# Retention in a two-model transformer kernel: from all-pairs scores to chunks of 128 tokens with carried states

## What is computed

```python
def retention_dir(q, k, v, log_gamma, include_diag):
    C = q.shape[-2]
    idx = jnp.arange(C, dtype=jnp.float32)
    rel = idx[:, None] - idx[None, :]
    ...
    decay_in = jnp.where(mask[None], jnp.exp(lg * jnp.maximum(rel, 0.0)[None]), 0.0)
    s = jnp.einsum('bhncd,bhnkd->bhnck', q, k) * decay_in[:, None]
    o_in = jnp.einsum('bhnck,bhnke->bhnce', s, v)
    k_dec = k * jnp.exp(lg * (C - 1 - idx)[None, :])...
    kv = jnp.einsum('bhncd,bhnce->bhnde', k_dec, v)
    ...
    def step(state, kv_n):
        return state * chunk_decay + kv_n, state
    ...
    q_dec = q * jnp.exp(lg * (idx + 1.0)[None, :])...
    o_x = jnp.einsum('bhncd,bhnde->bhnce', q_dec, s_prev)
    return o_in + o_x
...
    o = retention_dir(qc, kc, vc, log_decay[0], True) + flip(
        retention_dir(flip(qc), flip(kc), flip(vc), log_decay[1], False))
```

## Time and profile before

| | us |
|---|---|
| three runs, median (lowest to highest) | 3733.61 (3730.58 to 3734.66) |
| the profiled execution | 3733.86 |
| its span in the profile | 3732.0 |
| TensorE busy | 3615.1 (97%) |
| VectorE busy | 1887.5 (51%) |
| ScalarE busy | 1362.2 (36%) |
| GpSimd busy | 482.0 (13%) |
| mean granted TensorE clock | 0.991 of full |

### The profile page before, as it was taken

One profiled execution on the slowest core, in us unless ns is written; L12 is line 12 of the kernel. 1 busy time (PEld: TensorE's weight loads), 2 busy tenths in 40 slices (PEclk: granted clock), 3 DMA queues, 4 the chain that ended last, 5 costly groups with the idle time before them and its releaser, 6 DMA issues. The chain is left out here.

```text
span 3732.0 us, 58501 instructions
## 1 busy us (share of the span) xinstructions
PE 3615.1 (97%) x24178; PEld 3178.2 (85%) x24178; DVE 1887.5 (51%) x3312; ACT 1362.2 (36%) x2629; POOL 482.0 (13%) x586
## 2 busy tenths in 40 slices
PE   7999999999999999999999999999998999999998
PEld 6788778888888887888899889999997976888887
DVE  4555556565535556544455664433436556344444
ACT  3445444122224444322422452442233236244232
POOL 1222211000012432000110100110013110011001
PEclk9999999999999999999999999999999999999999
DMA  5111121333322212233311113222221111332332
GB/s 192 63 69 53 69 90 63 130 119 119 119 85 72 60 55 66 91 96 96 112 52 46 49 52 97 83 86 90 89 83 51 46 57 40 99 96 88 96 96 74
DMA packets 88248, 306.72 MB, mean 82 GB/s; under 512 B 10016, under 2 KB 13216, under 8 KB 87728
## 3 DMA queue, kind: packets, MB, share of 16 engines
q1 hardware_dynamic: 85184, 293.25, 24.5%
q0 software_dynamic: 2800, 9.73, 0.8%
HBM read 300.84 MB, written 2.10 MB: 81 GB/s over the span
## 5 line engine op out<-in xcount | busy, mean ns | idle before, releaser
L1944 DVE TENSOR_TENSOR weight_lo<-weight_raw,weight_hi 128x1024 fp32r<-128x1024 f32 (+1 forms) x464 | 561.4, 1213 | 431.9 <-ACT weight_hi L1344 431.3
L1344 ACT ACTIVATE weight_hi<-weight_raw 128x1024 fp32r<-128x1024 f32 (+1 forms) x464 | 476.7, 1031 | 587.9 <-PE bank L621 358.3
L621 PE MATMUL bank<-h_hi,weight_hi 128*128 128x512 f32 (+1 forms) x1288 | 469.1, 364 | 18.5 <-DVE h_lo L2387 9.1
L621 PE MATMUL bank<-h_lo,weight_hi 128*128 128x512 f32 (+1 forms) x1288 | 453.0, 352 | 0.0
L621 PE MATMUL bank<-h_hi,weight_lo 128*128 128x512 f32 (+1 forms) x1288 | 452.8, 352 | 0.0
L621 PE MATMUL bank<-u_hi,weight_hi 128*128 128x272 f32 (+2 forms) x1392 | 433.5, 311 | 3.0 <-DVE weight_lo L1944 2.1
L621 PE MATMUL bank<-u_lo,weight_hi 128*128 128x272 f32 (+2 forms) x1392 | 422.9, 304 | 0.0
L621 PE MATMUL bank<-u_hi,weight_lo 128*128 128x272 f32 (+2 forms) x1392 | 422.2, 303 | 0.0
L2810 POOL TENSOR_TENSOR scratch<-scratch 128x256 f32<-128x256 f32 (+2 forms) x132 | 113.8, 866 | 2020.5 <-ACT scratch L1382 2016.6
L621 PEld LDWEIGHTS bank<-h_hi,weight_hi 128*128 128x128 f32 x1288 | 245.9, 191 | 72.2 <-issue 31.2
L621 PEld LDWEIGHTS bank<-u_hi,weight_hi 128*128 128x128 f32 x1392 | 264.2, 190 | 30.4 <-issue 17.1
(11 more groups left out here) (319 smaller groups left out, 7983.7 us busy)
## 6 DMA issues: line engine op xcount, KB each, us to landing
weight_raw<-in_w_mlp SPq DMA_DIRECT2D x128, 512.0 KB, 3.6
weight_raw<-in_w_ff SPq DMA_DIRECT2D x128, 512.0 KB, 3.5
weight_raw<-in_w_in SPq DMA_DIRECT2D x92, 512.0 KB, 3.6
weight_raw<-in_w_mod SPq DMA_DIRECT2D x80, 512.0 KB, 4.4
weight_raw<-in_a_w_qkv SPq DMA_DIRECT2D x24, 512.0 KB, 3.9
weight_raw<-in_b_w_qkv SPq DMA_DIRECT2D x24, 512.0 KB, 3.6
first_weight<-in_w_mod SPq DMA_DIRECT2D x16, 512.0 KB, 15.2
weight_raw<-in_w_ret_o SPq DMA_DIRECT2D x16, 512.0 KB, 3.5
```

What stands on the lines that cost most here:

```text
L621: m = e.matmul(view[:, 0:hi - lo], a[:, k, :], b[:, k0 + k, lo:hi], start=(k == 0 and i == 0), stop=(k == kt - 1 and i == 2))
L1344: e.activation(whi[s % N_SPLIT][:, 0:kt, :], raw[n % N_RAW][:, 0:kt, :], ACT.Copy).then_inc(*tick("act_split", ("hi", n)))
L1944: e.tensor_tensor(wlo[s][:, 0:kt, :], raw[n % N_RAW][:, 0:kt, :], whi[s][:, 0:kt, :].bitcast(F32), ALU.subtract).then_inc(*tick("dve_split ...
```

## The change

Scores are computed only within a chunk: key tile j against its own 128 queries (16 for the meta tile). What lies between chunks goes through states. Per unit and direction ("way" 0 forward, 1 backward):

- `ret_turn` (TensorE): five transposes bring the keys of both heads to tokens in partitions.
- `ret_keys` (VectorE): three operations multiply them by their decays into KD and KDM.
- `ret_states` (TensorE): per chunk, way and head a matmul with the decayed keys stationary (64 columns wide) and the values moving; four chunks forward, and four (layer 0) or three (layer 1) backward.
- `ret_queries` (VectorE): three operations in layer 0, two in layer 1 make decayed queries QD, from factors QT that ScalarE makes in `query_decay`.
- `ret_states` (VectorE): eight (seven) operations in two chains, state i = state i-1 times the decay of a chunk plus the matmul's result.
- `ret_values` (TensorE): per chunk a matmul of the chunk's own scores (128 rows), then for each state that reaches it and each head a matmul of 64 rows with the state stationary.

The decays of a head shrink to 128 x 128, made after the fourth `fill()`. The six `fill()` calls of a unit stay, but stand between other parts. The constant table that is loaded is 624 columns narrower.

```diff
+                def ret_turn(g):
+                    e.wait_ge(*at("rr", layer, g, 1))
+                    for part, tiles in enumerate((ROW_TILES[0:4], ROW_TILES[4:5])):
...
+                            m = e.transpose(view[:, P * i:P * i + P], RK[:, g % 2, lo:lo + P], ident)
...
                 def ret_scores(g, span):
...
-                    for j, (k0, nk) in enumerate(ROW_TILES):
-                        views = [take("rs", layer, g, span, j, s) for s in range(2)]
+                    views = [take("rs", layer, g, span, s) for s in range(2)]
+                    for j, lo, n in tiles:
                         for s in range(2):
                             r = slice(HD * s, HD * s + HD)
-                            e.matmul(views[s][:, 0:hi - lo], RK[r, b, k0:k0 + P], RQ[r, b, lo:hi], start=True,
+                            m = e.matmul(views[s][:, lo - first:lo - first + n], RK[r, b, lo:lo + P],
+                                         RQ[r, b, lo:lo + n], start=True, stop=True)
...
+                def ret_states(g):
+                    b = g % 2
+                    e.wait_ge(*at("rvd", layer, g, 2))
+                    e.wait_ge(*at("kd", layer, g))
+                    for way, chunks in enumerate(((4, 0, 1, 2), (3, 2, 1, 0)[0:4 - layer])):
...
+                                m = e.matmul(view[c, P * i:P * i + P], key,
+                                             RV[b][0:P if j < 4 else N_META, j, P * s:P * s + P], start=True, stop=True)
...
+                def ret_values(g, span):
+                    first = tok.spans[span][0]
+                    views = [take("ro", layer, g, span, s) for s in range(2)]
+                    for s in range(2):
+                        e.wait_ge(*at("sd", layer, g, span, s))
+                    for way in range(2):
+                        e.wait_ge(*at("state", layer, g, way))
+                    e.wait_ge(*at("qd", layer, g))
+                    for j, lo, n in ret_tiles(layer, span):
+                        o = slice(lo - first, lo - first + n)
+                        for s in range(2):
+                            e.matmul(views[s][:, o], RV[g % 2][0:n, j, P * s:P * s + P], SD[0:n, span, s, o],
+                                     start=True, stop=False)
+                        ways = [(0, j)] * (j < 4) + [(1, 3 if j == 4 else 2 - j)] * (j != 3)
+                        for way, i in ways:
+                            for s in range(2):
+                                r = slice(HD * s, HD * s + HD)
+                                m = e.matmul(views[s][:, o], STATE[r, way, i, :], QD[r, way, lo:lo + n],
+                                             start=False, stop=(way, i) == ways[-1])
...
                 def ret_units(g, fill):
+                    ret_turn(g)
                     ret_scores(g, 0)
                     if g:
                         ret_broadcast(g - 1, 1)
...
-                    ret_values(g, 0)
+                    ret_states(g)
                     ret_scores(g, 1)
                     fill()
+                    ret_values(g, 0)
+                    fill()
                     ret_statistics(g, 0)
+                    ret_values(g, 1)
                     fill()
                     ret_broadcast(g, 0)
-                    fill()
-                    ret_values(g, 1)
                     fill()
                     ret_statistics(g, 1)
                     fill()
```

VectorE's unit, and the chain of states in it:

```diff
                 def ret_units(g, fill):
+                    ret_keys(g)
                     ret_decay(g, 0)
                     if g:
                         ret_normalise(g - 1, 1)
-                    if g < 3:
-                        decay_strip(2 * g + 2)
                     fill()
+                    ret_queries(g)
+                    ret_states(g)
                     ret_decay(g, 1)
+                    fill()
                     fill()
                     ret_variance(g, 0)
                     fill()
                     ret_normalise(g, 0)
-                    if g < 3:
-                        decay_strip(2 * g + 3)
-                    fill()
+                    for h in range(2 * g + 2, 2 * g + 4 if g < 3 else 0):
+                        decay_strip(h)
...
+                            if i == 0:
+                                e.tensor_scalar(STATE[:, way, 0, :], view, 1.0, None, ALU.mult).then_inc(
+                                    *tick("dve_attn", *done))
+                            else:
+                                e.wait_ge(*at("state", layer, g, way))
+                                e.scalar_tensor_tensor(
+                                    out=STATE[:, way, i, :], in0=STATE[:, way, i - 1, :],
+                                    scalar=CD[:, 4 * way + g:4 * way + g + 1], in1=view, op0=ALU.mult,
+                                    op1=ALU.add).then_inc(*tick("dve_attn", *done))
```

More of the change, by code:

```diff
@@ L478, in ret_var, with ret_tiles @@
             return RVAR[:, c:c + 6].rearrange("p (s t) -> p s t", s=2)
+        def ret_tiles(layer, span):
+            return [(j, *ROW_TILES[j]) for j in ([4] if (layer, span) == (0, 0) else []) + [2 * span, 2 * span + 1]]
         def ret_before(layer, g, span):
@@ L1126, in gate_retention @@
                     yield from product_T(("rg", layer, m_), (w_in, 16 + m_), U_HI, U_LO, wide(layer), ready)
+                def ret_turn(g):
+                    e.wait_ge(*at("rr", layer, g, 1))
+                    for part, tiles in enumerate((ROW_TILES[0:4], ROW_TILES[4:5])):
+                        job = ("kt", layer, g, part)
+                        view = take(*job)
+                        for i, (lo, _) in enumerate(tiles):
+                            m = e.transpose(view[:, P * i:P * i + P], RK[:, g % 2, lo:lo + P], ident)
+                        m.then_inc(*tick("pe_turn", job))
+                        close(*job)
@@ new lines, in ret_states @@
+                def ret_states(g):
+                    e.wait_ge(*at("cd", layer))
+                    for s in range(2):
+                        e.wait_ge(*at("ro", layer, g - 1, 1, s))
+                    for i in range(4):
+                        for way in range(2):
+                            last = 3 - layer * way
+                            if i > last:
+                                continue
+                            job = ("st", layer, g, way)
+                            view = view_of(*job)[:, P * i:P * i + P]
+                            e.wait_ge(*at(*job))
+                            done = [("state", layer, g, way)] + [("free", *job)] * (i == last)
+                            if i == 0:
[7 more added lines that the diff above has]
+                                    op1=ALU.add).then_inc(*tick("dve_attn", *done))
@@ L3010, in ret_units @@
                     for span in range(2):
-                        fill()
-                        fill()
+                        for _ in range(2 + (span == 0)):
+                            fill()
                         e.wait_ge(*at("rvar", layer, g, span))
```

174 lines of the change are left out of this document (126 added, 48 removed).

## The result

| | before | changed | ratio, 95% interval |
|---|---|---|---|
| median of the first comparison, us | 3732.9 (3730.6 to 3734.7) | 3695.1 (3691.0 to 3696.4) | 0.9895 [0.9883, 0.9908] |
| profiled execution, us | 3733.9 | 3696.2 | |
| span, us | 3732.0 | 3694.4 | |

Faster by 1.05%, 38 us where 43.4 were forecast.

A forecast was written before the change was run, and what follows sets the result against it. TensorE's stream was taken to bound the kernel: 120.3 us less 1.0 leaves, 75.9 us is added, a gain of 43.4 us. From 3733.9 that gives 3690.5, stated as 3690.0 us, range 3680 to 3706.

The forecast's parts named there:

- The bound: Both retention stages: TensorE's stream sets the time at upper clock, so time leaving it leaves the total absent new waits.
- The sum: Retention stages: TensorE work removed less work added, a gain of 43.4 us.
- What goes, 120.3 us: Old scores and values on TensorE in eight units: their busy times, 120.3 us, leave.
- The check by edges: Old scores and values, start to start plus group edges: 14.28 us, some 14.8 a unit, about 120 us in all.
- The 1.0 us that I reserved: First scores of layer 1: about 1 us is a bank VectorE frees late; the following product will meet it.
- What is added, 75.9 us: New TensorE work: pairs 34.3 us, full-array matmuls 15.8, transposes 4.4, switches of array tiling 21.4.
- A single matmul's latency as the drain: Alternative switch price from the skill page, some 166 ns drain: switches near 30 us, gain near 35, time near 3699.
- The signs: Expected in the changed profile: windows about 184 and 157 us, scores and values about 9.5 a unit, values 3.6 and 2.3.
- Rival 1: First values wait for VectorE's chain of states: 1 to 2 us a unit, 3698 to 3706 us; chance 0.13.
- Rival 2: New matmuls' stationary loads no longer hidden: 40 us more if none are, 3730 us, no measurable change; chance 0.04.
- Rival 3: TensorE waits every unit for keys, states, values chain; slower once the wait passes 5.4 us a unit; chance 0.02.
- What I costed at nothing: VectorE's and ScalarE's new work, PSUM banks, the smaller constant table and other stages: covered or unchanged, no added time.

The follow-up runs named there:

- second and third run: The changed kernel, unaltered, timed twice more beside the kernel before: medians 3689.4 and 3689.9 us, ratios 0.9885 and 0.9883.
- the queries six times: Changed kernel with VectorE computing the decayed queries six times instead of once, five into buffers nobody reads: 3700.7 us.
- Own chunk only: Changed kernel without the products of states and decayed queries, so nothing crosses from one chunk to another: 3665.5 us.
- the queries nine times: Changed kernel with VectorE computing the decayed queries nine times instead of once, eight into buffers nobody reads: 3746.8 us, ratio 1.0037 to the kernel before.
- the fill ahead of the transposes: Changed kernel with the first fill of products moved ahead of transposes and first scores in each layer's first unit: 3689.0 us.

## Why the prediction was right, and what was mis-sized

- **The bound.** Right: TensorE was busy for every microsecond of both windows, and the span fell by what left its stream (37.8 and 37.6 us).
- **The sum.** Forecast 43.4 us, found 37.8 in the windows: 5.6 short. The lengths of the units say where. The six units behind the first ones gave 28.9 us (4.27, 4.23 and 4.18 in layer 0, 5.40, 5.41 and 5.38 in layer 1), where the terms of the prediction, taken unit by unit, make 30.5. The two first units and the products ahead of them gave 8.9 us, where its terms make 12.8.
- **What goes, 120.3 us: right but for the first units.** In a unit behind the first the busy sum is what leaves. The check by edges came out low (14.28 and 0.2 us): the last value matmul reaches 0.19 us into the products, as the first of them takes 0.31 us from start to start (2016.27 to 2016.58) and not 0.12, and 0.09 is the entry, 14.76 in all. In the first units the scores were longer because the clock was at 0.50: from start to start their groups took 15.19 and 16.86 us, where 14.28 and 13.95 are usual. I let these 3.8 us leave with the matmuls, but for 1.0. But such a stretch does not leave with the matmuls that stand in it: it was 3.4 + 6.8 us long before and is 6.8 + 6.8 in the first run of the changed kernel, and slows transposes and products instead. The 3.4 us more cost **1.7 us**; in the second and third run they are not there. This is the term that was most mis-sized. The 1.0 us that I reserved as a wait for a bank was also misread: the row has 0.20 us of waiting, and the rest is this clock.
- **What is added, 75.9 us: some 2.5 us too small.** From start to start a unit has 9.97 us in layer 0 and 8.55 in layer 1. With four exits of 0.1 us and entries of 0.09 us (two in layer 0, one in layer 1), that is 10.55 and 9.04 us, 78.4 in all; against 14.76 and 14.43 before, this gives the 4.2 and 5.4 us by which the units are shorter. Full-array instructions at 0.111 and switches at 0.20 were measured within 0.005 us of what I took, and pairs at 0.107 (single starts give 0.112). What I did not count is the border between the meta keys' states (16 rows) and the others (128 rows), a switch once in each unit: the starts there are 0.20 and 0.16 us apart instead of 0.11, 0.15 us more, 1.2 us in all. A single matmul's latency as the drain, the estimate that the prediction makes from the page TensorE: Matmul & The Clock Gate of the Trainium skill (Single matmul latency), would have meant some 0.27 us a switch; the measured 0.20 us decides for the rows.
- **The signs.** The changed windows are 187.0 and 159.0 us, for 184 and 157 forecast. Values: 3.44 and 2.33 us for 3.6 and 2.3. Scores and values of a unit: 9.3 us on average from start to start, 9.8 with the edges that the forecast of 9.5 included.
- **How much of it is luck.** The later comparisons, 41.7 and 43.8 us below the kernel before, lie closer to 43.4 than the sum deserves: in the stages the change gives 40.2 and 39.5 us there, and the rest of the difference lies in stages that the change leaves alone.
- **Rival 1, VectorE late at the first values:** not there, no wait, and 2.6 to 3.5 us of slack in the eight units. The run with the queries six times shows that it was near: 4 us more on the chain and it begins.
- **Rival 2, loads not hidden:** refuted. Own chunk only has full-array instructions at 0.111 us and pairs at 0.107. In its trace full-array instructions of only 16 moving columns also start 0.112 us apart, which is then the load; and in the trace of before those of 256 columns start 0.216 us apart, so that 128 columns of stream are some 0.108 us. The rule of the Trainium skill (TensorE: Matmul & The Clock Gate, What overlaps and what doesn't), by which a load hides only behind matmuls on other rows of the array, is not what these full-array matmuls show: 0.111 us holds one load or one stream, not one after the other.
- **Rival 3, slower by a wait in each unit:** not there, but its price was wrong. I put the break-even at a wait of 5.4 us in each unit. The run with the queries nine times is slower than before with 3.7 us on average. A long wait costs the clock behind it as well: 29.5 us of waits made 47.7 in the stages.
- **What I costed at nothing:** right for keys, queries, states and weights, which no row of TensorE's waits in the units names. No wait for banks is right as well; it stops being so as soon as the second scores come earlier.

## What to carry to other kernels

Take what a removed group is worth from a unit at full clock, by its busy sum or from start to start with every edge, and check it against the whole length of the unit; leave a stretch of low clock out of it, since here the stretch stayed when the matmuls in it went. Count the changes between full array, row halves, column halves and 16 rows as work of their own (0.20 us here between the larger ones, as much as two instructions of 128 columns), and group by kind; but when work moves earlier, move its consumer too, or the bank it holds takes the gain back. A long wait of TensorE, here of 3.6 us and more, is dearer than its length: in all six cases the matmuls behind it ran at half clock for a while.

## What was not expected

The price of long waits: of 47.7 us that the repeated queries cost, 29.5 were waiting and 18.2 the same matmuls at the lower clock. The waits for states of up to 2.8 us left the clock alone. The second surprise is the 16 rows: going from 16 to 128 rows of the full array is a switch too, at 0.18 us among the values and 0.15 among the states.

**The clock and the spread of one kernel.** TensorE's granted clock has two levels here, 1.00 (2.4 GHz) and 0.50 (1.2 GHz). Windows of the changed kernel, first run: the last products ahead of the first unit of layer 0, the low stretch in that unit, the one in layer 1, and one in a stage that the change leaves alone:

```profile
1880.80:1887.60 6.80, 6.80 (x62) 6.80 (x60) 2.96 (x7) 1.90 (x2) 0.44 (x1) 1.00 0.01 4
...
1887.70:1894.50 6.80, 6.80 (x36) 6.25 (x36) 6.38 (x19) 0.00 (x1) 1.02 (x2) 0.50 0.04 5
2836.60:2843.40 6.80, 5.60 (x27) 5.05 (x28) 6.49 (x22) 0.00 (x0) 1.53 (x2) 0.50 0.01 3
...
1150.40:1153.80 3.40, 3.40 (x9) 2.63 (x8) 1.23 (x1) 0.11 (x1) 3.40 (x2) 0.50 0.73 208
```

36 matmuls in the second window, 62 in the first. Just before both retention stretches stand the row sums, 20 matmuls of a single column, over 2.2 us in layer 0; in layer 1 waits of 0.9 and 1.7 us stand beside them. Twelve of the thirteen traces have the stretch in layer 0, whatever follows the row sums, and all have the one in layer 1. Each such 3.4 us at the lower level costs 1.7 us where TensorE is busy. The traces have them in all stages: 81.6 us in the first run of the changed kernel, 70.2 in the second and 57.6 in the third. Half the first difference, 5.7 us, is about the 5.3 us between the spans (3694.4 and 3689.2); half the second, 6.3 us, is more than the 3.1 us to the third span (3686.1). So this clock is the likely cause of the 6 us between the medians, but that is not shown. The gain of the change itself is better read from the stages: 38.2 us in the first run, 39.9 without its 1.7 us of additional low clock, and 40.2 and 39.5 in the others, all against one trace of before. What makes the stretch in layer 0 last 0, 3.4 or 6.8 us stays open; the fill ahead of the transposes did not settle it.
